# A one-core transformer block on Trainium2: the second half of x loaded later, and transposed between the row tiles of the first projection

## The reference, cut to what matters

```
c_act = silu(c)
mod   = c_act @ ada_w + ada_b           # 6 vectors of 1024: shift1, scale1, gate1, shift2, scale2, gate2
h     = rms_norm(x, norm1_g) * (1 + scale1) + shift1
u     = h @ w_in                        # first the differential attention's queries (512 columns), then its keys, ...
lam   = exp(sum(lq1*lk1)) - exp(sum(lq2*lk2)) + lambda_init
... attention, gated linear attention, gated merge, w_out, mixture of 32 experts
```

## Time and profile before

| | before |
|---|---|
| median of 3 runs | 1624.14 us (1623.71 to 1625.76) |
| the profiled execution: its own time | 1627.21 us |
| the profiled execution: span | 1625.4 us |
| mean granted clock of PE | 0.97 |
| PE busy | 1532.3 us, 94% of the span |
| DVE, ACT, POOL busy | 527.9, 354.9, 111.5 us |
| last of group 0's slices ends on DVE | 39.42 us |
| first product of section 0 | 49.77 us |
| section 1 ends on PE | 162.12 us |

### The profile page before, as it was taken

How to read it: one execution, slowest core, us unless ns; L and a number is a source line. 1 busy time by engine, 2 the same in 40 slices (tenths; PEclk the granted TensorE clock), 3 DMA queues, 4 the chain that set the end, 5 groups by cost and what they waited for, 6 DMA issues and landing times.

```text
span 1625.4 us, 20666 instructions
## 1 busy us (share of the span) xinstructions
PE 1532.3 (94%) x8167; PEld 687.2 (42%) x8167; DVE 527.9 (32%) x1087; ACT 354.9 (22%) x691; POOL 111.5 (7%) x141
## 2 busy tenths in 40 slices
PE   3999999999999999999999999769999999998996
PEld 3444545454545555444444455424333333332332
DVE  6746322323232224722222255552111111111110
ACT  4212322222223712121111133311011110110110
POOL 1000000000000000000000000101111111111111
PEclk9899899999999999999999999879999999999998
DMA  9940101010001001011130653348999999999993
GB/s 365 347 178 0 52 1 52 1 52 0 26 13 26 14 27 27 26 39 39 39 116 0 252 226 112 152 180 314 358 400 408 405 406 413 406 410 412 405 384 80
DMA packets 67886, 290.96 MB, mean 179 GB/s; under 512 B 11444, under 2 KB 36063, under 8 KB 52447
## 3 DMA queue, kind: packets, MB, share of 16 engines
q1 hardware_dynamic: 60912, 273.08, 42.3%
q0 software_dynamic: 6896, 16.79, 4.1%
HBM read 276.74 MB, written 20.45 MB: 183 GB/s over the span
## 4 chain that ended last, share of the span: by engine, by line
PE 52%; DMA 5%; DVE 2%; issue 0%; ACT 0%; POOL 0%; SPq 0%; POOLq 0%; DVEq 0%
PE PS L648 50%; DMA R<-in_expert_w 2%; DMA HT<-in_expert_w 2%; PE PS L1025 1%; PE PS L1047 1%; DMA out_rows<-R 1%; PE PS L969 0%; DVE R L1391 0%; DVE R L1388 0%; DVE WK L1383 0%; ACT R L1118 0%; DVE R L1387 0%; DVE R L1383 0%; PE PS L900 0%; DVE WK L1388 0%
## 5 line engine op out<-in xcount | busy, mean ns | idle before, releaser
L648 PE MATMUL PS<-R 128*32 128x512 f32 (+5 forms) x4136 | 767.6, 579 | 21.2 <-ACT R L1118 8.9
L648 PEld LDWEIGHTS PS<-R 128*32 128x32 f32 (+3 forms) x4136 | 266.8, 128 | 403.9 <-issue 383.7
L648 PE MATMUL PS<-R,HT 128*128 128x512 f32 (+1 forms) x768 | 342.7, 603 | 4.0 <-DVE HT L1388 3.3
L648 PE MATMUL PS<-HT,R 128*32 128x512 f32 (+2 forms) x1184 | 324.4, 608 | 4.9 <-DMA R<-in_expert_w 3.2
L1383 DVE TENSOR_TENSOR R<-R,PS 128x512 f32<-128x512 f32 (+1 forms) x96 | 72.7, 774 | 470.0 <-PE PS L648 470.0
L648 PEld LDWEIGHTS PS<-R,HT 128*128 128x128 f32 x768 | 145.5, 193 | 176.5 <-issue 175.1
L1118 ACT ACTIVATE R<-PS 128x512 f32<-128x512 f32 (+4 forms) x130 | 78.0, 608 | 427.0 <-PE PS L648 282.8
L648 PEld LDWEIGHTS PS<-HT,R 128*32 128x32 f32 (+1 forms) x1184 | 108.1, 134 | 142.6 <-issue 140.6
L648 PE MATMUL PS<-WK,R 128*32 128x512 f32 (+1 forms) x464 | 92.2, 593 | 0.0
L612 POOL DMA_INDIRECT out_rows<-R x40 | 57.6, 1440 | 323.0 <-DVE R L1391 159.3
L1118 ACT ACTIVATE R<-PS,S,A 128x128 f32<-128x128 f32 x92 | 34.6, 456 | 189.0 <-PE PS L1025 189.0
(11 more groups left out here) (231 smaller groups left out, 854.0 us busy)
## 6 DMA issues: line engine op xcount, KB each, us to landing
R<-in_expert_w SPq DMA_DIRECT2D x67, 2048.0 KB, 27.0
HT<-in_expert_w SPq DMA_DIRECT2D x20, 2048.0 KB, 21.6
R<-in_ada_w SPq DMA_DIRECT2D x24, 1024.0 KB, 7.4
WK<-in_expert_w SPq DMA_DIRECT2D x9, 2048.0 KB, 29.5
R<-in_w_in SPq DMA_DIRECT2D x6, 2048.0 KB, 8.1
R<-in_w_in SPq DMA_DIRECT2D x16, 512.0 KB, 4.7
R<-in_x SPq DMA_DIRECT2D x2, 2048.0 KB, 11.1
R<-in_x SPq DMA_DIRECT2D x8, 512.0 KB, 4.0
```

What stands on the lines that cost most here:

```text
L648: return nc.tensor.matmul(o, l, r, start=a, stop=z)
```

## The change

The order of the loads becomes: c, slice 0, the eight small ones, slice 1, the first half of x, slices 2 to 7, the first weights, the second half of x, the small ones, and the rest as before. The multiplication of the first half of x by its reciprocal roots moves from DVE to ACT; that of the second half stays on DVE, behind the scaling of the first half of hT. PE transposes row tiles 0 to 3 before the sums of group 0 as it did, and row tiles 4 and 5 behind row tile 1 of section 0, row tiles 6 and 7 behind row tile 2. ACT squares the second half after it has scaled the first half of hT, and scales the second half after it has copied row tile 7. DVE scales its part of the second half behind slice 3 of group 1. A fill of `acc` with zeros on DVE moves behind the first two slices. The diff, cut to what acts:

```
@@ SP: the queue of loads
-            load_x(0)
+            load_ada(0, 0, False)
             e.wait_ge(s["fills_done"], 1)
...
-            for j in range(2):
-                load_ada(0, j, False)
-            load_x(1)
+            load_ada(0, 1, False)
+            load_x(0)
             for j in range(2, KT):
                 load_ada(0, j, False)
             e.dma_start(wring[:, 0], w_in_v[:, :, O_DQ:O_DQ + HW]).then_inc(s["w_ld"], 16)
+            load_x(1)
             small(acc[0:1, 1:3, :], vec("ada_b")[:, 2048:6144].rearrange("a (g n) -> a g n", g=2))
@@ TensorE
-            for t in range(NT):
+            def turn_x(t):
                 e.wait_ge(s["x_norm"], t + 1)
-                e.wait_ge(s["h_eva"], t + 1)
+                e.wait_ge(s["h_eva"], t + 1 + t // 4)
                 for k in range(KT):
...
+            for t in range(4):
+                turn_x(t)
             e.wait_ge(s["ada_done"], KT)
...
-            project(0, True)
+            e.wait_ge(s["w_ld"], 16)
+            for t in range(NT):
+                if t % 4 == 0:
+                    e.wait_ge(s["h_evd"], 1 + t // 4)
+                    e.wait_ge(s["h_eva"], 7 + 5 * (t // 4))
+                project(0, t)
+                if t in (1, 2):
+                    turn_x(2 * t + 2)
+                    turn_x(2 * t + 3)
             e.wait_ge(s["small_ld"], 16 * N_SMALL)
-            project(1)
+            e.wait_ge(s["w_ld"], 32)
+            for t in range(NT):
+                project(1, t)
@@ ScalarE
-            for g in range(2):
+            def squares(g):
                 e.wait_ge(x_ld[g], 16)
...
-            for t in range(NT):
+
+            def h_raw(t):
                 e.wait_ge(s["x_tr"], t + 1)
...
-            e.wait_ge(s["mod1_done"], 2)
-            e.wait_ge(s["h_eva"], 2 + NT)
-            for half in range(2):
+            def h_scaled(half):
+                e.wait_ge(s["h_eva"], 6 + 5 * half)
                 c = slice(half * 512, (half + 1) * 512)
                 for k in range(5, KT):
                     last = act(hT[:, k, c], hT[:, k, c], ACT.Identity, scale=A1[:, k:k + 1], bias=S1[:, k:k + 1])
                 last.then_inc(s["h_eva"], 1)
+
+            squares(0)
+            e.wait_ge(s["rs_ready"], 1)
+            for t in range(4):
+                act(x_all[:, t, :], x_all[:, t, :], ACT.Copy, scale=xstat[:, 0, t:t + 1]).then_inc(s["x_norm"], 1)
+            for t in range(4):
+                h_raw(t)
+            e.wait_ge(s["mod1_done"], 2)
+            h_scaled(0)
+            squares(1)
+            for t in range(4, NT):
+                h_raw(t)
+            h_scaled(1)
             e.wait_ge(s["lam_done"], 1)
             act(lam[:, 2:4], lam[:, 0:2], ACT.Exp).then_inc(s["lam_done"], 1)
@@ VectorE
-            v.memset(acc[:, 1:3, :], 0.0)
             e.wait_ge(s["cact_1"], 1)
...
-            def normalise(g):
+            def x_roots(g):
                 e.wait_ge(s["sd_ready"], g + 1)
                 v.reciprocal(xstat[:, 0, 4 * g:4 * g + 4], xstat[:, 1, 4 * g:4 * g + 4]).then_inc(s["rs_ready"], 1)
-                e.wait_ge(s["rs_ready"], g + 1)
-                for t in range(4 * g, 4 * g + 4):
-                    tsc(x_all[:, t, :], x_all[:, t, :], xstat[:, 0, t:t + 1], ALU.mult).then_inc(s["x_norm"], 1)
-
-            normalise(0)
+
+            v.memset(acc[:, 1:3, :], 0.0)
             ada(0, 2)
             ada(0, 3)
-            normalise(1)
+            x_roots(0)
             for j in range(4, KT):
                 ada(0, j)
...
-            e.wait_ge(s["h_eva"], 2 + NT)
-            for half in range(2):
+            def h_scaled(half):
+                e.wait_ge(s["h_eva"], 6 + 5 * half)
...
+            h_scaled(0)
+            x_roots(1)
+            e.wait_ge(s["rs_ready"], 2)
+            for t in range(4, NT):
+                tsc(x_all[:, t, :], x_all[:, t, :], xstat[:, 0, t:t + 1], ALU.mult).then_inc(s["x_norm"], 1)
...
-            with e.Fori(1, 3) as g:
-                for j in range(KT):
-                    ada(g, j)
+            for j in range(4):
+                ada(1, j)
+            h_scaled(1)
+            for j in range(4, KT):
+                ada(1, j)
+            for j in range(KT):
+                ada(2, j)
```

More of the change, by code:

```diff
@@ L665, in _, with project @@
             last.then_inc(s["mod1_ps"], 1)
-            def project(n, first=False):
-                e.wait_ge(s["w_ld"], 16 * (n + 1))
-                for t in range(NT):
[L672 to L679, removed]
-            project(0, True)
+            def project(n, t):
+                e.wait_ge(s["proj_free"], n * NT + t + 1)
+                for k in range(KT):
+                    last = mm(bank(t % 4), hT[:, k, t * P:(t + 1) * P], wring[:, n % 2, k, :], k == 0, k == KT - 1)
+                last.then_inc(s["proj_mm"], 1)
+            e.wait_ge(s["w_ld"], 16)
[7 more added lines that the diff above has]
+                    turn_x(2 * t + 3)
             e.wait_ge(s["small_ld"], 16 * N_SMALL)
-            project(1)
+            e.wait_ge(s["w_ld"], 32)
+            for t in range(NT):
+                project(1, t)
             e.wait_ge(s["ada_done"], 3 * KT)
```

## The result

The changed kernel takes 1637.3 us, median of 6 runs (1635.76 to 1638.75), against 1624.13 for the kernel before (6 runs, 1623.71 to 1626.2). The ratio is 1.0077, 95% interval 1.0064 to 1.009: slower by 13.2 us. The profiled execution took 1636.06 us.

A forecast was written before the change was run, and what follows sets the result against it. PE, busy 94% of the span, bounds the kernel, with DVE and the loads setting its start. -7.1 - 3.0 + 3.6 + 15.6 + 2.4 = +11.5 on 1627.21 gives 1638.7, or 1635.6 us for the median; range 1632.5 to 1640.5.

The forecast's parts named there:

- The earlier last slice: Start, DVE and loads: group 0's last slice ends at 32.3 us against 39.42, -7.1 us.
- The clock in the sums: PE's small sums of group 0: they find the clock the transposes leave, full instead of half, -3.0 us.
- the sums stay slow: Rival for group 0's sums: clock not risen or without effect, that term 0, total +14.5, 1638.6 us; chance 0.22.
- The turned row tiles: PE in section 0: four row tiles transposed between products, 0.9 us each at full clock, +3.6 us.
- The stall: PE before row tile 4: idle for DVE's scaling of the second half, itself held at `lam_done`, +15.6 us.
- The signs listed at the end of the prediction: Expected profile: among others, DVE waits about 17 us for lam and PE about 15.6 us for hT.
- The clock behind the stall: PE from row tile 4: the clock is at 0.50 again after the idle time, +2.4 us.
- Transposes always at the half clock: Rival for PE's transposes: sums term 0, four turned tiles 7.4 us, total +18.3, 1642.4 us; chance 0.06.
- The loads come late: Rival for the start: last slice gains 4 us rather than 7.1, total +14.6, 1638.7 us; chance 0.09.
- DVE isn't held: Rival: no DVE wait at `lam_done`, second half scaled right behind row tile 7's copy, -6.1, 1618.0 us; chance 0.03.

The follow-up runs named there:

- the last experiment: Changed kernel with the first half of x loaded ahead of slices 0 and 1 again and DVE's fill first again: 1638.07 us, against 1625.78 before.
- third experiment: Changed kernel with the multiplication of the first half of x back on DVE instead of ACT: 1640.26 us, 14.7 above the kernel before.
- the busy stall: Changed kernel with 132 transposes of the identity put into PE's wait before row tile 4: median 1639.57 us, 14.0 above the kernel before.
- the 26 behind the sums: Changed kernel with 18 identity transposes before the sums of group 0 and 26 after: 1635.91 us, 2.1 below the changed kernel of its set.

## Why the prediction was right

The forecast was 1635.6 us in a range of 1632.5 to 1640.5, slower with a chance of 0.95; measured were 1637.3 and, later, 12.6 above the kernel before. By its terms:

**The earlier last slice, -7.1:** -7.8 (the sums start at 31.68 against 39.48). Slice 2 came at 16.84 rather than 17.4 and DVE was never kept waiting long. The reason was only half right: the place of the slices ahead of x is worth nothing (the last experiment); the second half of x out of the way and the multiplications out of DVE's way are what moved it. With the first half multiplied on DVE, the gain would be 2.6 us smaller (third experiment).

**The clock in the sums, -3.0:** this is the term that was mis-sized. The mechanism is there in part: the sums do begin at the full clock, and with transposes ahead of them they took 3.73 us in two profiles, though 5.45 in a third. But the forecast had the clock stay up through them, and it falls under them: -2.3 in the first profile, -1.2 on the mean of seven. The forecast also had the sums 1 us behind the last transpose, which was to end near 31.4; it ended at 29.2 and PE waited 2.50 us. The rival "the sums stay slow" (term 0) is at least as near as the forecast: the mean of -1.2 is closer to it, and so is the median of 1637.3, to its 1638.6 by 1.3 us and to 1635.6 by 1.7.

**The scaling, not named:** PE waits 2.99 us for it instead of 3.30, -0.3.

**The turned row tiles, +3.6:** 3.5 in the trace, and doubling them added 3.2 to 3.5.

**The stall, +15.6:** 15.08 in the changed kernel, nothing with the exponential earlier, 5.4 without the four slices. Each link of the chain stood where it was put: copy of row tile 7, three scalings, table and exponential, the angles, four slices, five scalings. The signs listed at the end of the prediction had DVE wait "about 17 us" for lambda; its own working, from 48 us to 5.0 us behind row tile 7 (about 66), gives some 23, and 22.03 were measured. The 15.6 did not rest on that number.

**The clock behind the stall, +2.4:** 2.0, by the one traced execution of the busy stall.

With the measured terms, -7.8 - 1.2 - 0.3 + 3.5 + 15.1 + 2.0 = +11.3. That this comes so near the forecast's +11.5 is in part luck: the sums brought 1.8 us less than forecast, and the last slice (0.7), the stall (0.5), the clock behind it (0.4), the scaling (0.3) and the turned row tiles (0.1) together made up for it. The trace up to the end of section 1 has +10.6 in one profile (sums of 4.71) and 174.10 - 162.12 = +12.0 in the other (sums of 6.70). The medians differ by 12.6 to 13.2. The 1 to 2 us between are not located. Behind section 1 the span is 1461.6 and 1462.9 us long in the two profiles of the changed kernel and 1463.3 in the one of the kernel before, and it lies between 1461.5 and 1463.1 in the profiles of all the versions above, so the changes do not show there by more than the spread. The profiled execution of the kernel before (1627.21) was 3 us above its median, and where it lost them is not known; the differences against its trace are open by as much. No give-back further on was forecast, and none is seen.

**The rivals.** "Transposes always at the half clock" is refuted: the pairs in section 0 took 1.75 us at the full clock, the 132 in the stall ran at 1.00, and under the 26 behind the sums the clock rose from 0.50 (0.94 in 40 to 41). The Trainium skill ("TensorE: Matmul & The Clock Gate", section "Part 4: PE-mode transpose") says that transposes do not bring on the full clock. The measurements here disagree with it, and they decide. "The loads come late" did not happen. "DVE isn't held" is the changed kernel with the exponential moved, and it ends on the other side, 1619.8 to 1620.5 with 1625.7 before; its forecast of 6.1 us below the kernel before compares with 5.3 to 5.8. Like the main sum, it has the sums too short and the last slice too late.

## What to carry to other kernels

When work is put later on one engine, follow every wait that stands in front of it and behind it in the other streams: here a tiny exponential, unrelated to the moved work, was queued behind it on ACT, DVE was queued behind the exponential, and PE behind DVE. An operation that others wait for and that depends on little belongs ahead of the first long wait of its stream; moving these two lines turned 13 us lost into 5 to 6 gained. And price the parts apart: one multiplication moved to an idle engine, with no load reordered, brought 4.4 by itself.

## What was not expected of the hardware

The granted clock falls while PE is busy, if what it does is products of one column. The clearest rows are those of the second set of such products, behind section 1 (their weights are read with a stride). In the changed kernel PE comes to it from products of 512 columns at 1.00 and without idle time:

```profile
176.12 7.53 PE L648 MATMUL PS<-onesf,R 128*128 128x1 f32 x32
```

```profile
178.00:180.00 2.00, 2.00 (x10) 1.00 1.01 377
180.00:182.00 2.00, 2.00 (x10) 0.75 0.02 5
182.00:184.00 2.00, 2.00 (x8) 0.50 0.00 0
```

The same fall stands within this set in all fourteen profiles. In the sums of group 0 the clock went to 0.50 at about 34 in one execution of the changed kernel and 32 in another, and the same 32 instructions took from 4.7 to 7.0 us. Transposes of 128x128 held it at 1.00 in the stall of one execution (14.57 us of them, behind products of 512 columns) and bring it up again (26 that began at 0.50, with row tile 0 behind them at 1.00). They do not hold it always: in the two profiles with sums of 3.73 us it fell under the transposes right behind the sums, with PE never idle in between. That the one-column products ahead of them are the reason is likely and not shown.

The Trainium skill ("TensorE: Matmul & The Clock Gate", section "Part 1: The HAM clock gate") says that the moment at which the clock rises varies between runs of one kernel. Here it is the fall whose moment varies, as the spread of the sums shows.
